# Seven block products from pair 5 on instead of pair 6 in the stages up1 and up2

## What is computed

```python
D_MODEL = 1024
SEQ = 512
D_FF = 2816

def swiglu(x, w_gate, w_up, w_down):
    return (jax.nn.silu(x @ w_gate) * (x @ w_up)) @ w_down
...
        h = h + 0.5 * swiglu(rms_norm(h, ffn1_norm[l]), ffn1_w_gate[l], ffn1_w_up[l], ffn1_w_down[l])
...
        h = h + 0.5 * swiglu(rms_norm(h, ffn2_norm[l]), ffn2_w_gate[l], ffn2_w_up[l], ffn2_w_down[l])
```

## Time and profile before

| what | us |
|---|---|
| median of 3 runs | 2024.47 (2024.34 to 2024.7) |
| the profiled execution, its own time | 2023.55 |
| its span, from the first to the last instruction | 2021.8 |
| TensorE (PE) busy in the span | 2004.9 |
| VectorE (DVE) busy | 1459.2 |
| ScalarE (ACT) busy | 986.8 |

### The profile page before, as it was taken

One profiled execution on the slowest core, in us unless ns is written; L12 is line 12 of the kernel. 1 busy time (PEld: TensorE's weight loads), 2 busy tenths in 40 slices (PEclk: granted clock), 3 DMA queues, 4 the chain that ended last, 5 costly groups with the idle time before them and its releaser, 6 DMA issues.

```text
span 2021.8 us, 32634 instructions
## 1 busy us (share of the span) xinstructions
PE 2004.9 (99%) x12670; PEld 1757.3 (87%) x12670; DVE 1459.2 (72%) x2427; ACT 986.8 (49%) x1607; POOL 244.3 (12%) x266
## 2 busy tenths in 40 slices
PE   9999999999999999999999999999999999999998
PEld 7999988778899988988788899988877798999887
DVE  7988833786888863587778988833667879988733
ACT  5555622354445542453454655622557754555522
POOL 0000000500000000000002122000536520122001
PEclk9999999999999999999999999999999999999999
DMA  8322233322232223321321677333256624666232
GB/s 263 120 105 105 84 102 106 133 67 84 84 105 105 100 87 99 106 105 63 95 84 69 166 186 185 101 102 112 106 138 170 165 71 136 172 183 173 86 99 70
DMA packets 90141, 236.99 MB, mean 117 GB/s; under 512 B 47728, under 2 KB 51104, under 8 KB 73616
## 3 DMA queue, kind: packets, MB, share of 16 engines
q1 hardware_dynamic: 72896, 184.04, 27.8%
q0 software_dynamic: 14768, 37.49, 8.5%
q10 hardware_dynamic: 2336, 13.52, 2.0%
HBM read 211.86 MB, written 7.38 MB: 108 GB/s over the span
## 4 chain that ended last, share of the span: by engine, by line
PE 92%; DVE 5%; POOL 1%; ACT 1%; issue 1%; DMA 0%; SPq 0%; DVEq 0%; POOLq 0%
PE ps L1285 29%; PE ps L1286 28%; PE ps L1287 28%; DVE act L2557 1%; PE ps L512 1%; PE ps L525 1%; PE ps L718 1%; PE ps L736 1%; PE ps L703 1%; DVE w_lo L1794 1%; DVE w_lo L1784 0%; PE ps L1262 0%; PE ps L1272 0%; PE ps L1307 0%; DVE g_exps L792 0%
## 5 line engine op out<-in xcount | busy, mean ns | idle before, releaser
L1794 DVE TENSOR_TENSOR w_lo<-raw,w_hi 128x2048 fp32r<-128x2048 f32 (+3 forms) x144 | 287.7, 1998 | 153.8 <-ACT w_hi L1766 145.6
L1285 PE MATMUL ps<-act,w_hi 128*128 128x512 f32 (+1 forms) x1026 | 376.2, 367 | 2.7 <-DVE w_lo L1794 1.6
L1286 PE MATMUL ps<-act,w_hi 128*128 128x512 f32 (+1 forms) x1026 | 371.8, 362 | 0.0
L1287 PE MATMUL ps<-act,w_lo 128*128 128x512 f32 (+1 forms) x1026 | 371.8, 362 | 0.0
L1285 PE MATMUL ps<-xq,w_hi 128*128 128x256 f32 x1024 | 290.2, 283 | 1.4 <-DVE w_lo L1794 1.0
L1286 PE MATMUL ps<-xq,w_hi 128*128 128x256 f32 x1024 | 289.8, 283 | 0.0
L1287 PE MATMUL ps<-xq,w_lo 128*128 128x256 f32 x1024 | 289.7, 283 | 0.0
L1285 PEld LDWEIGHTS ps<-act,w_hi 128*128 128x128 f32 x1026 | 193.5, 189 | 40.3 <-issue 7.9
L1287 PEld LDWEIGHTS ps<-act,w_lo 128*128 128x128 f32 x1026 | 193.6, 189 | 30.4
L1286 PEld LDWEIGHTS ps<-act,w_hi 128*128 128x128 f32 x1026 | 193.7, 189 | 28.8
L1285 PE MATMUL ps<-xq,w_sum_hi 128*128 128x256 f32 x768 | 217.6, 283 | 0.5 <-ACT up L2010 0.5
(11 more groups left out here) (301 smaller groups left out, 3978.8 us busy)
## 6 DMA issues: line engine op xcount, KB each, us to landing
raw<-in_w_up SPq DMA_DIRECT2D x87, 1024.0 KB, 4.8
raw<-in_w_down SPq DMA_DIRECT2D x29, 768.0 KB, 4.2
raw<-in_w_in SPq DMA_DIRECT2D x20, 1024.0 KB, 4.8
raw<-in_w_down SPq DMA_DIRECT2D x29, 640.0 KB, 3.8
raw<-in_w_out SPq DMA_DIRECT2D x8, 1024.0 KB, 4.8
w_sum<-in_w_up POOLq DMA_DIRECT2D x32, 256.0 KB, 4.4
raw<-raw POOLq DMA_DIRECT2D x32, 256.0 KB, 3.3
w_sum_odd<-in_w_up POOLq DMA_DIRECT2D x32, 256.0 KB, 4.5
```

The costliest lines, as they stand in the source:

```text
L1285: pe.matmul(own, hi, rhs_hi, start=start, stop=False, skip_group_check=more)
L1286: pe.matmul(own, hi, rhs_lo, start=False, stop=False, skip_group_check=more)
L1287: return pe.matmul(own, lo, rhs_hi, start=False, stop=stop, skip_group_check=more)
L1794: eng.tensor_tensor(w_lo[:, w], raw[:, w], w_hi[:, w].bitcast(F32), ALU.subtract).then_inc(lo_rounded, 1)
```

## The change

`PLAIN` becomes a table by stage: 5 for up1 and up2, 6 for up3 and up4 as before. In up1 and up2 pair 5 is done with seven products, so the x side, the weight sums of pair 5 and those of pair 6 are placed one pair sooner. In the first seven-product pair VectorE's rests for the next pair move behind the addition into `up`. For up3 and up4 the emitted order stays as it was.

```diff
-PLAIN = 6
+PLAINS = {"up1": 5, "up2": 5, "up3": 6, "up4": 6}
...
+        def plain(st):
+            return PLAINS[st.name]
+
+        def first_seven(a):
+            return sum(KF - PLAINS[name] for name in SEVEN[:a])
...
                     if st.name in SEVEN:
-                        for i in range(PLAIN // 2):
+                        for i in range(plain(st) // 2):
                             body(i)
-                        for f in range(PLAIN, KF):
+                        if plain(st) % 2:
+                            body(plain(st) // 2, u=1)
+                        for f in range(plain(st), KF):
                             seven_pe(st, f)
...
             def plain_act(st, f, f0):
...
-                if f == PLAIN - 3:
-                    round_quarters(a, 0 if conv else 2)
-                if f == PLAIN - 2:
-                    round_sum(st, PLAIN, 1)
-                    round_sum(st, PLAIN, 2)
-                if f < PLAIN - 1 and not (conv and f == 0):
+                if f == plain(st) - 3:
+                    round_quarters(a, 0)
+                if f == plain(st) - 2:
+                    round_sum(st, plain(st), 1)
+                    round_sum(st, plain(st), 2)
+                if f < plain(st) - 1 and not (conv and f == 0):
                     silu(f, f0)
-                if f == PLAIN - 4 and not conv:
-                    round_quarters(a, 0, 1)
-                if f == PLAIN - 3:
-                    round_quarters(a, 1 if conv else 3)
+                if f == plain(st) - 3:
+                    round_quarters(a, *((1,) if conv else (1, 2, 3)))
...
             def plain_dve(st, f, f0):
...
-                if f == PLAIN - 4 and not conv:
-                    rest_quarters(st, 0)
-                if f == PLAIN - 3:
+                if f == plain(st) - 3:
                     if not conv:
-                        rest_quarters(st, 1)
-                    sum_pair(st, PLAIN)
-                    fourth_sum(st, PLAIN)
-                    rest_quarters(st, 0 if conv else 2)
-                if f == PLAIN - 2:
-                    rest_quarters(st, 2 if conv else 3)
-                    rest_sum(st, PLAIN, 1)
+                        rest_quarters(st, 0)
+                    sum_pair(st, plain(st))
+                    fourth_sum(st, plain(st))
+                    rest_quarters(st, 0 if conv else 1)
+                if f == plain(st) - 2:
+                    rest_quarters(st, 2)
                     if not conv:
-                        rest_sum(st, PLAIN, 2)
-                        sum_pair(st, PLAIN + 1)
-                        fourth_sum(st, PLAIN + 1)
+                        rest_quarters(st, 3)
+                    rest_sum(st, plain(st), 1)
+                    if not conv:
+                        rest_sum(st, plain(st), 2)
+                        sum_pair(st, plain(st) + 1)
+                        fourth_sum(st, plain(st) + 1)
...
             def seven_dve(st, f, f0):
...
-                rest_weights(eng, st.q0 + nxt, 0, 0)
-                if more:
+                if f > plain(st):
+                    rest_weights(eng, st.q0 + nxt, 0, 0)
+                if f > plain(st) and more:
                     rest_sum(st, nxt, 0)
...
                 eng.tensor_tensor(up[:, HALF:T], ra, prod[:, HALF:T], ALU.add).then_inc(fourth_ready, 1)
+                if f == plain(st):
+                    rest_weights(eng, st.q0 + nxt, 0, 0)
+                    rest_sum(st, nxt, 0)
```

More of the change, by code:

```diff
@@ L1593, in seven_pe @@
                 pe.wait_ge(fourth_ready, n + 1)
-                if f == PLAIN:
+                if f == plain(st):
                     pe.wait_ge(xq_ready, rests + 4)
@@ L2014, in round_act @@
                 a = SEVEN.index(st.name)
-                last = (KF - PLAIN) * (a + 1) - 1
+                last = first_seven(a + 1) - 1
                 if f < 4:
@@ L2060, in seven_act @@
                 nxt, a = f + 1, SEVEN.index(st.name)
-                if f < PLAIN:
+                if f < plain(st):
                     plain_act(st, f, f0)
@@ L2066, in seven_act @@
                 more = nxt < KF
-                conv, first = st.evac == "conv", f == PLAIN
-                if conv and f > PLAIN + 1:
+                conv, first = st.evac == "conv", f == plain(st)
+                if conv and f > plain(st) + 1:
                     silu(f - 1, f0)
@@ L2071, in seven_act @@
                 keep(prod[:, 0:HALF], ra, 6 * n + 1)
-                if conv and f == PLAIN + 1 or first and not conv:
+                if conv and f == plain(st) + 1 or first and not conv:
                     silu(f - 1, f0)
@@ L2622, in conv_dve @@
                     sum_pair(st, nxt)
-                if f > PLAIN:
+                if f > plain(st):
                     gated_product(st, f - 1, f0)
@@ L2630, in conv_dve @@
                 eng.tensor_tensor(shifted[:, 2:2 + HALF], rc, prod[:, 0:HALF], ALU.add)
-                if f > PLAIN:
+                if f > plain(st):
                     rest_weights(eng, st.q0 + nxt, 0, 0)
-                if f > PLAIN and more:
+                if f > plain(st) and more:
                     rest_sum(st, nxt, 0)
@@ L2639, in conv_dve @@
                 eng.wait_ge(seven_done, 6 * n + 5)
-                wait(eng, prod_ready, f0 + f if f > PLAIN else f0)
+                wait(eng, prod_ready, f0 + f if f > plain(st) else f0)
                 eng.tensor_tensor(up[:, HALF:T], ra, prod[:, HALF:T], ALU.add).then_inc(fourth_ready, 1)
@@ L2724, in seven_dve @@
                 gated_product(st, f - 1, f0)
-                if more and f > PLAIN:
+                if more and f > plain(st):
                     sum_pair(st, nxt)
@@ L2730, in seven_dve @@
                 eng.tensor_tensor(gate[:, 0:HALF], rc, prod[:, 0:HALF], ALU.add)
-                rest_weights(eng, st.q0 + nxt, 0, 0)
-                if more:
+                if f > plain(st):
+                    rest_weights(eng, st.q0 + nxt, 0, 0)
+                if f > plain(st) and more:
                     rest_sum(st, nxt, 0)
-                else:
+                if not more:
                     for j in range(3):
```

52 lines of the change are left out of this document (25 added, 27 removed).

## The result

The changed kernel takes 2037.18 us (median of 4 runs, 2036.34 to 2037.8) against 2024.4 us for the kernel before on the same chip: a ratio of 1.0064 [1.0051, 1.0076]. It is 12.8 us slower, and the forecast was 2037.1.

What follows compares the result with a forecast made beforehand. It took TensorE as the bound, VectorE's list as a second hidden by 0.9 us. up1 +6.4 and up2 +4.5 gave +10.9, median 2035.4; one clock fall at 1.7 made 2037.1, range 2034.3 to 2040.0.

Steps and rivals of the forecast that it cites:

- the case that gave 2037.1: Waits plus one fall of the clock, in up1 where the gap is longest: 2035.4 + 1.7; chance 0.40.
- The bound and the mechanism: VectorE's list makes the last plain `gate` late; ScalarE's silu and rounding precede the copy into `up`; `gate` at 71.59, 556.5.
- The waits: TensorE in pair 5 waits at quarter 5, 6.17 us in up1 and 4.3 in up2; at quarter 3, 0.3.
- The sum with the clock unchanged: Saving and waits in the openings of up1 and up2: +6.4 and +4.5, together +10.9 us.
- The small terms, 0.2 and 0.8: TensorE waits in pair 6 of each stage: 0.2 us at its start for `w_lo`, 0.8 at quarter 5.
- The clock: Idle gaps in up1 and up2 may halve TensorE's rate; net price of a fall 1.7 us.
- The case of two falls: Waits, and a fall of the clock in both up1 and up2: 2038.8; chance 0.22.
- the gross price of 2.4: Work lost per clock fall, 2.4 us, read from the slow pace at the program's start; 0.7 of it given back.
- the saving in the sum, 0.80: One pair each in up1 and up2 becomes seven-product: 10.88 - 10.08 = 0.80 us per stage, 1.6 in all.
- keeps quarter 7 from waiting: In the first seven-product pair, moving `w_lo` behind the addition into `up` spares quarter 7 a wait, priced at 0.2 and 0.8.
- The lag is not worked off: Rival: the 0.8 us wait repeats in the 15 pairs behind pair 6, 24 us more, 2059; chance 0.03.
- The other side: Rival: x side and sums fit into five pairs, copy into `up` never late, only the saving left: 2022.9; chance 0.07.

Runs made afterwards that it cites:

- e_keep: Changed kernel with ScalarE's copy into `up` and the copy behind it ahead of silu and rounding in the first seven-product pair; 2029.71 us.
- e_warm: Changed kernel with 40 (up1) and 28 (up2) extra unread TensorE matmuls of 256 columns ahead of quarter 5 of pair 5; 2034.28 us.
- e_wlo: Changed kernel with `w_lo` and the first sum rest back ahead of the addition into `up` in the first seven-product pair; 2035.5 us.
- e_pool: Changed kernel with weight additions for pairs 5 and 6 of up1 and up2 on GpSimd, and ScalarE's copies ahead of silu and rounding; 2031.61 us.
- e_pool_only: Changed kernel with the weight additions for pairs 5 and 6 of up1 and up2 done by GpSimd instead of VectorE; 2036.49 us.

## Why the prediction came out right

The waits and what makes them came as laid out. That the time came within 0.1 us is luck: the case that gave 2037.1 (one fall of the clock) isn't the one that happened.

**The bound and the mechanism** held. VectorE's list gives the time: the last plain `gate` was forecast 8.30 us behind the start of pair 5 in up1 (71.59 - 63.29) and came 8.29 behind it (72.32 - 64.03); in up2, forecast 6.45 and came at 6.42. e_keep shows the other half, ScalarE's order: with the copies first the long wait is gone.

**The waits** held. At quarter 5, forecast 6.17 and 4.3, measured 6.00 and 4.12; at quarter 3, forecast 0.3, measured 0.3 (the matmul ahead of it began at 66.78, and the next at 67.22 where 0.12 is the pace). The copy ended 3.41 us behind the start of the `gate` (forecast 3.48).

**The sum with the clock unchanged** can be held against e_warm, where the clock did not change. up1: -0.80 + 6.01 + (11.02 - 10.08) + 0.2 for the last quarters of pair 6 is +6.35, forecast +6.4. up2: -0.80 + 4.14 + 0.92 + 0.2 is +4.5, forecast +4.5. The median of e_warm lies 10.3 above that of before in the same session, where 10.9 was forecast. The small terms, 0.2 and 0.8, can be read in that kernel only (1.1 in each stage); in the changed one they are mixed with the clock's.

**The clock** is where the step was wrong, twice, and the two errors nearly cancel. The forecast took one fall, in up1, at 1.7 us net; there were two, at 1.24 each. The case of two falls, which I gave 0.22, is what happened; its 2038.8 is 1.6 above the median, by these prices: two times 1.7, less two times 1.24, is 0.9, and 0.6 is the difference between the 10.9 of the sum without the clock and the 10.3 of e_warm. The term that was mis-sized is the gross price of 2.4, taken from the start of the program: in the changed kernel the rest of pair 5 took 1.75 and 1.48 us more than 4.32, of which 0.1 is the longer first matmul, so the clock lost some 1.65 and 1.4, and 0.4 and 0.2 of it came back, where I had 0.7. In e_wlo, behind gaps of the same length, the slow stretches were longer and cost 2.7 and 2.2, about the 2.4 of the forecast; what sets their length these runs don't settle. In up2 I judged the gap of 4.1 us nearer to the fall at the end of the program, and it was: the last matmul there began at 564.0, and the clock was at 1.00 until after 567. A fall shortly before the gap's end cost nearly as much here as one in its middle (1.4 and 1.65), since the time until the clock is back is paid in work. The Trainium skill (TensorE: Matmul & The Clock Gate, section Why this matters for your kernels) says that idle gaps between bursts of matmuls put the array back to half rate; the prediction left open whether it would hold here, and the trace agrees, with 0.50 in both gaps. Its section Back-to-back issue gap gives N / 1.2 GHz from one matmul to the next while slow, 213 ns for 256 columns; the rows at 76.17 and 76.38 are 0.21 apart. The section gives this, and the formula for full speed from which the prediction's estimate of 1.2 us is worked out, for an isolated matmul and not for a stream with weight loads; the saving in the sum, 0.80, was rightly taken from rows.

**One claim was not borne out, without touching the number**: that the new place of `w_lo` "keeps quarter 7 from waiting". e_wlo has the old place and no wait at quarter 7, with the clock low; at the full clock, by the estimate above, it would be 0.3 us. The new place is behind the 1.1 us of small waits that each stage has at the full clock (e_warm). I had worked out what the new place costs and not what the old one would.

**The rivals.** "The lag is not worked off" is refuted by the pace of 10.08 in pair 7. "The other side" needed a `gate` 6.2 us sooner than laid out; it came where it was laid out. That the saving of 0.80 us per stage is real, no run shows by itself: it is the small term beside every wait, and in e_keep, the best order tried, three waits of together 3.5 us in up1 and 2.1 in up2 still outweigh it.

## What to carry to other kernels

A cheaper unit of work whose operands another engine prepares is worth its saving only as long as that engine's list ends in time: before moving the switch, lay out the preparing engine's list from start to start and compare its end with the new due time, since here 0.8 us per stage was to be had and a margin of 0.9 us had to cover a due time that moved 10.88 against a list that moved 4.0. A wait of several microseconds on TensorE can cost more than its length: in each profiled execution with a gap of 4.0 to 5.5 us the granted clock fell in it or just behind it, and the work behind ran at half rate for 2.8 to 5.9 us. Gaps of up to 2.6 us (e_keep, e_pool, and up2 of e_pool_only) didn't bring it down there. And in an engine that executes in order, the instruction that the bound engine waits for should not stand behind one that waits for a late input: that reordering alone gave back 7.5 of the 12.8 us, the clock's share included.

## What the runs showed of the hardware

That GpSimd and VectorE hold each other up in whole instructions was not expected. The rows of e_pool fit an order in which one finishes before the other starts: VectorE's `w_lo` ends at 51.63, and GpSimd's addition that had been started at 49.48 ends 1.16 us behind that, at 52.79, near its 1.29 alone; VectorE's `act`, started at 51.55, ends at 53.34, 0.55 behind GpSimd's end. In the same way GpSimd's last addition takes 3.22 beside an x rest. The Trainium skill (SBUF — State Buffer, section SBUF: two separate sides) describes this as an exclusive lock on a port pair that a VectorE instruction with two inputs in SBUF and a GpSimd instruction that reads SBUF both need, taken for the whole instruction; these rows agree. An experiment that measures this by itself, with GpSimd's additions added to a kernel that doesn't need them, was not run.
